# Seven block products per tile of the up projection, and the down projection as a pass of its own

## What is computed

```
u = rmsnorm(x, norm_ffn) @ ffn_w_up                  # 1024 -> 2 x 2816
u_pad = concatenate([buf0, u], axis=1)
uc = sum(u_pad[:, j:j + T] * wc[j] for j in range(3)) + ffn_conv_b
gate, up = split(uc, 2, axis=-1)
x = x + (silu(gate) * up) @ ffn_w_down               # 2816 -> 1024
x = x + sigmoid(rmsnorm(x, ple_norm) @ ple_w_gate) * (p_in @ ple_w_proj)
```

## Time and profile before

| | |
|---|---|
| median of 3 runs | 3063.3 us |
| the profiled execution | 3064.34 us |
| its span, first to last instruction | 3062.5 us |
| mean granted TensorE clock | 0.982 |
| PE / DVE / ACT / POOL busy in the span | 2942.2 / 1581.2 / 1136.7 / 141.3 us |
| matmul records | 19219 |

### The profile page before, as it was taken

How to read it: one execution, slowest core, us unless ns; L and a number is a source line. 1 busy time by engine, 2 the same in 40 slices (tenths; PEclk the granted TensorE clock), 3 DMA queues, 4 the chain that set the end, 5 groups by cost and what they waited for, 6 DMA issues and landing times. The chain is left out here.

```text
span 3062.5 us, 46703 instructions
## 1 busy us (share of the span) xinstructions
PE 2942.2 (96%) x19219; PEld 2779.4 (91%) x19219; DVE 1581.2 (52%) x2699; ACT 1136.7 (37%) x2151; POOL 141.3 (5%) x260
## 2 busy tenths in 40 slices
PE   6999989999999999999989998899999999999997
PEld 5998745999999999999989986569999999999997
DVE  5234644664544555457661446455645554455665
ACT  6233333543333223335452342344432233333353
POOL 0000300000000000000000003000000000000000
PEclk9999999999999999999999989999999999999998
DMA  3101153321111111112221022533211111111121
GB/s 131 42 28 68 73 172 118 140 74 42 44 54 42 42 55 42 56 47 83 91 72 42 17 107 84 162 103 126 74 42 42 56 42 56 42 42 46 43 98 70
DMA packets 70742, 215.40 MB, mean 70 GB/s; under 512 B 6522, under 2 KB 43386, under 8 KB 54146
## 3 DMA queue, kind: packets, MB, share of 16 engines
q1 hardware_dynamic: 70530, 212.42, 20.1%
HBM read 193.52 MB, written 18.87 MB: 69 GB/s over the span
## 5 line engine op out<-in xcount | busy, mean ns | idle before, releaser
L236 PE MATMUL psum<-h_chunk,out_weight_parts 128*128 128x352 f32 x2112 | 681.5, 323 | 0.0
L237 PE MATMUL psum<-h_chunk,out_weight_parts 128*128 128x352 f32 x2112 | 677.1, 321 | 0.0
L238 PE MATMUL psum<-h_chunk,out_weight_parts 128*128 128x352 f32 x2112 | 676.4, 320 | 0.0
L2257 DVE SCALAR_TENSOR_TENSOR conv_sum<-u_padded,vectors,conv_sum 128x1024 f32<-128x1024 f32 x176 | 226.3, 1286 | 540.5 <-ACT conv_sum L2109 537.4
L237 PEld LDWEIGHTS psum<-h_chunk,out_weight_parts 128*128 128x128 f32 x2112 | 396.8, 188 | 0.0
L236 PEld LDWEIGHTS psum<-h_chunk,out_weight_parts 128*128 128x128 f32 x2112 | 396.2, 188 | 0.0
L238 PEld LDWEIGHTS psum<-h_chunk,out_weight_parts 128*128 128x128 f32 x2112 | 395.8, 187 | 0.0
L236 PE MATMUL psum<-g_parts,out_weight_parts 128*128 128x352 f32 x960 | 309.3, 322 | 0.0
L237 PE MATMUL psum<-g_parts,out_weight_parts 128*128 128x352 f32 x960 | 309.0, 322 | 0.0
L238 PE MATMUL psum<-g_parts,out_weight_parts 128*128 128x352 f32 x960 | 308.8, 322 | 0.0
L2283 DVE TENSOR_TENSOR x<-x,psum 128x352 f32<-128x352 f32 x528 | 254.8, 519 | 94.4 <-PE psum L238 94.1
(11 more groups left out here) (360 smaller groups left out, 5420.9 us busy)
## 6 DMA issues: line engine op xcount, KB each, us to landing
out_weight_stage<-w_up_dram SPq DMA_DIRECT2D x44, 1024.0 KB, 4.7
out_weight_stage<-w_down_dram SPq DMA_DIRECT2D x22, 1024.0 KB, 4.7
mix_weight_stage<-w_in_dram SPq DMA_DIRECT2D x18, 1024.0 KB, 4.9
pages<-cache_dram SPq DMA_DIRECT2D x64, 288.0 KB, 4.3
out_weight_stage<-w_out_dram SPq DMA_DIRECT2D x16, 1024.0 KB, 6.8
out_weight_stage<-w_gate_dram SPq DMA_DIRECT2D x16, 1024.0 KB, 4.7
pages<-cache_dram SPq DMA_DIRECT2D x64, 160.0 KB, 2.6
x<-x_in_dram SPq DMA_DIRECT2D x6, 1408.0 KB, 11.2
```

The lines of the kernel that those rows point to most:

```text
L236: pe.matmul(out, lhs[0], rhs[0], start=first, stop=False)
L237: pe.matmul(out, lhs[0], rhs[1], start=False, stop=False)
L238: return pe.matmul(out, lhs[1], rhs[0], start=False, stop=last)
L2257: dve.scalar_tensor_tensor(t[:, q, 0:SEQ], row[:, tap:tap + SEQ], w, t[:, q, 0:SEQ], ALU.mult, ALU.add).then_inc(ph["conv_step"], 1)
```

## The change

**Up projection.** Tile 0 stays an ordinary product, but in 8 groups of the column slices 264, 264, 176 and 352 (`first`). For tiles 1 to 21 the product (2 x 128 rows of gate and up) x (1024 features) x (1056 tokens) is cut in two along each of the three dimensions and made from 7 block products instead of 8, a Strassen-Winograd scheme. A block product is 4 k-tiles x 3 matmuls, for each of two 264-column halves s: 24 matmuls. Four of them use sums of weight blocks (S1 to S4) and of activation blocks (T1 to T4). The T are made once per layer, in place in X, by DVE (`t_sum`), and split by ACT and DVE (`t_high`, `t_low`). The S are made per tile by POOL (`sums`), for tile 1 by DVE (`weight_sums`). Results are put together by ACT (`m1`, `corner`) and DVE (`u2`, `u3`, `c22`, `c21`, `c12`), partly by going on accumulating in the same bank. The taps are now read from u in SBUF (`taps`), u has two buffers, and the convolution of tile f - 1 runs during tile f.

**Down projection.** The gated rows go to DRAM tile by tile (`store_g`). After the last tile a separate pass goes over chunks c and output tiles t_, with all 22 k-tiles in one accumulation (`down`, 16 units of 33 matmuls per chunk, weights loaded anew for each chunk: 48 loads of 704 KB per layer). X, overwritten by the T, is stored before (`keep`) and loaded back for this pass. The order of the first four units is 0, 2, 1, 3.

**Rope scores.** All plain matmuls of a query block come first, then all rope matmuls. The slab of SBUF grows (SLAB 50304 to 54144 words), and the DMA scratch is set to 1024.

The core of the diff:

```diff
-                    w = min(512, keys - c)
-                    out = [ps[:, 2 * b + c // 512, 0:w] for b in range(2)]
+                slices = [(c, min(512, keys - c)) for c in range(0, keys, 512)]
+                for c, w in slices:
                     for b in range(2):
-                        pe.matmul(out[b], qn[:, h0 + b, queries], kn[:, h0 + b, c:c + w], start=True, stop=False)
+                        pe.matmul(ps[:, 2 * b + c // 512, 0:w], qn[:, h0 + b, queries], kn[:, h0 + b, c:c + w],
+                                  start=True, stop=False)
+                for c, w in slices:
                     for b in range(2):
-                        mm = pe.matmul(out[b], qr[part(b), h0 // 2, queries], kr[part(b), c:c + w],
-                                       start=False, stop=True)
+                        mm = pe.matmul(ps[:, 2 * b + c // 512, 0:w], qr[part(b), h0 // 2, queries],
+                                       kr[part(b), c:c + w], start=False, stop=True)
                         if c + w == keys:
                             mm.then_inc(ph["s_done"], 1)
 
...
+            def product(f, i, s, a, x, begin):
+
+                at, out = slice(s * SUB, (s + 1) * SUB), bank(i, s)
+                for k in range(KH):
+                    w = [unit(slot_of(f), a, q, k) for q in range(2)]
+                    parts = [part[:, k, at] for part in x]
+                    pe.matmul(out, w[0], parts[0], start=begin and k == 0, stop=False, skip_group_check=not begin)
+                    pe.matmul(out, w[0], parts[1], start=False, stop=False, skip_group_check=not begin)
+                    mm = pe.matmul(out, w[1], parts[0], start=False, stop=k == KH - 1, skip_group_check=not begin)
+                mm.then_inc(ph["m_done"], 1)
+
...
+            def up(f):
+                for a in product_order(f):
+                    if a == A11:
+                        pe.wait_ge(ph["w_lo_made"], 2 * f - 1)
+                    if a == S3:
+                        pe.wait_ge(ph["w_lo_made"], 2 * f)
+                        pe.wait_ge(ph["tlo_made"], 1)
+                    if a == S1:
+                        pe.wait_ge(ph["tlo_made"], 2)
+                    if a == S2:
+                        pe.wait_ge(ph["tlo_made"], 3)
+                    if a == A22:
+                        pe.wait_ge(ph["tlo_made"], 4)
+                    for s in range(2):
+                        made = 2 * (f - 1) + s + 1
+                        if a == A11:
+                            free(f, 0, s, "c11_made")
+                            product(f, 0, s, A11, block_of(0, 0), True)
+                        if a == S3:
+                            free(f, 2, s, "c21_made")
+                            product(f, 2, s, S3, t_block(T3), True)
...
+                            product(f, 1, s, S2, t_block(T2), True)
...
+                            product(f, 2, s, A22, t_block(T4), False)
+                        if a == S4:
+                            pe.wait_ge(ph["c22_made"], made)
+                            product(f, 3, s, S4, block_of(1, 1), False)
...
+            def down(d):
+                c, j = divmod(d, 2 * KX)
+                t_, half = divmod(UNIT_ORDER[j], 2)
+                if half == 0:
+                    if c:
+                        pe.wait_ge(ph["x_made"], KX * (c - 1) + t_ + 1)
+                    else:
+                        pe.wait_ge(ph[("c11_made", "u2_made", "c21_made", "c12_made")[t_ // 2]], 2 * LAST)
+                pe.wait_ge(ph["wd_lo_made"], d + 1)
+                w = wd[down_slot(d)]
+                for i in range(DK):
+                    k = half * DK + i
+                    if t_ == 0:
+                        pe.wait_ge(ph["glo_made"], groups_to(c, k))
+                    mm = product3(pe, ps[:, BANKS[t_], 0:CH], [w[:, q, i * P:(i + 1) * P] for q in range(2)],
+                                  [gd[c % 2][:, k, q, :] for q in range(2)], k == 0, k == FT - 1)
...
+            for f in range(1, FT):
+                up(f)
+            for d in range(2 * KX * NC):
+                down(d)
...
+            def sums(f):
+
+                slot, n = slot_of(f), 4 * (f - 1)
+                pool.wait_ge(ph["w_loaded"][slot], 32 * ((f - 1) // 2 + 1))
+                pool.wait_ge(ph["w_summed"], n)
+                if f >= 3:
+                    pool.wait_ge(ph["m_done"], m_before(f - 1))
+                pool.tensor_tensor(raw(slot, S1), raw(slot, S3), raw(slot, A22), ALU.add).then_inc(ph["w_summed"], 1)
+                pool.wait_ge(ph["w_summed"], n + 1)
+                pool.tensor_tensor(raw(slot, S2), raw(slot, S1), raw(slot, A11), ALU.subtract)\
+                    .then_inc(ph["w_summed"], 1)
+                pool.tensor_tensor(raw(slot, S3), raw(slot, A11), raw(slot, S3), ALU.subtract)\
+                    .then_inc(ph["w_summed"], 1)
+                pool.wait_ge(ph["w_summed"], n + 2)
+                pool.tensor_tensor(raw(slot, S4), raw(slot, A12), raw(slot, S2), ALU.subtract)\
+                    .then_inc(ph["w_summed"], 1)
 
...
+            for f in range(1, LAST):
+                store_g(f - 1)
+                if f + 2 < FT:
+                    sp.wait_ge(ph["m_done"], m_before(f) + 12)
+                    load_up(f + 2)
+            sp.wait_ge(ph["m_done"], m_before(LAST))
...
+            for c in range(NC):
+                sp.dma_start(X[:, :, chunk(c)], core.x_dram[:, :, chunk(c)]).then_inc(ph["x_back"][c], 16)
+            store_g(LAST)
...
+            t_high(T1)
+            t_high(T3)
+            first_evacuate(4)
+            first_evacuate(5)
+            t_high(T2)
+            first_evacuate(6)
+            first_evacuate(7)
+            t_high(T4)
+            act.wait_ge(ph["first_free"], FIRST_G)
+            taps(0, 1)
+            taps(0, 0)
+            for f in range(1, FT):
+                m1(f)
...
+                if f > 1:
+                    silu(f - 1)
...
+            def m1(f):
+                for s in range(2):
+                    act.wait_ge(ph["m_done"], done_after(f, A11, s))
+                    if f >= 2:
+                        act.wait_ge(ph["c12_made"], 2 * (f - 2) + s + 1)
+                    act.activation(part2[:, s], bank(0, s), ACT.Copy).then_inc(ph["m1_made"], 1)
+
...
+            def taps(f, q):
+                if f:
+                    act.wait_ge(ph["g_stored"][(f - 1) % 2], 16 * ((f - 1) // 2 + 1))
+                tile = f + q * FT
+                w2 = vec[:, ds1(tile * CONV_W + V_CW + CONV_W - 1)]
+                bias = vec[:, ds1(tile + V_CB)]
+                row = u[f % 2][:, q]
+                act.activation(t[:, q, 0:SEQ], row[:, 2:US], ACT.Identity, bias=bias, scale=w2)
+                act.activation(tokens(t[:, q, SEQ:NT]), samples(row)[:, :, CONV_W - 1:], ACT.Identity, bias=bias,
+                               scale=w2).then_inc(ph["taps_ready"], 1)
+
...
+            def t_sum(T):
+
+                n = T_ORDER.index(T)
...
+                dve.wait_ge(ph["nlo_made"], 16)
+                for j in range(0, KH, 2):
...
+                    if n:
+                        dve.wait_ge(ph["t_summed"], 2 * (n - 1) + j // 2 + 1)
+                    dve.tensor_tensor(rows((kh, out)), rows(left), rows(right), ALU.subtract)\
+                       .then_inc(ph["t_summed"], 1)
+
+            def t_low(T):
+                later = {T1: 3, T3: 2, T2: 4, T4: 4}
+                dve.wait_ge(ph["thi_made"], T_ORDER.index(T) + 1)
+                dve.wait_ge(ph["t_summed"], 2 * later[T])
+                dve.tensor_tensor(t_rows(tl, T), t_rows(X, T), th[:, T].bitcast(F32), ALU.subtract)\
+                   .then_inc(ph["tlo_made"], 1)
+
...
+            def u2(f, s):
+                dve.wait_ge(ph["m1_made"], 2 * (f - 1) + s + 1)
+                dve.wait_ge(ph["m_done"], done_after(f, S2, s))
+                dve.tensor_tensor(part2[:, s], part2[:, s], bank(1, s), ALU.add).then_inc(ph["u2_made"], 1)
+
+            def u3(f, s):
+                dve.wait_ge(ph["m_done"], done_after(f, S3, s))
+                dve.wait_ge(ph["u2_made"], 2 * (f - 1) + s + 1)
+                if f >= 2:
+                    dve.wait_ge(ph["c22_made"], 2 * (f - 1))
+                dve.tensor_tensor(part3[:, s], part2[:, s], bank(2, s), ALU.add).then_inc(ph["u3_made"], 1)
+
...
+            sums_low(1)
+            t_low(T3)
+            t_sum(T2)
+            t_low(T1)
+            t_sum(T4)
+            t_low(T2)
+            t_low(T4)
+            u2(1, 0)
+            u2(1, 1)
+            u3(1, 0)
+            u3(1, 1)
+            c22(1, 0)
+            c22(1, 1)
+            blocks_low(2)
+            dve.wait_ge(ph["zeroed"], 4)
...
+            for f in range(2, FT):
+                if f == 2:
+                    gated(0)
+                conv(f - 1, 1, 0)
+                conv(f - 1, 1, 1)
+                u2(f, 0)
+                conv(f - 1, 0, 0)
+                u2(f, 1)
+                conv(f - 1, 0, 1)
```

(3 more changed lines are left out.)

774 lines of the change are left out of this document (506 added, 268 removed).

## The result

The changed kernel takes 3032.2 us (median of 4, 3028.8 to 3036.4) against 3063.1: ratio 0.9899, 95% interval [0.9882, 0.9916]. It is faster, by 31 us where 67 were forecast, and 6 us outside the range. A second set of runs gave 0.9882 [0.9867, 0.9897].

The account below looks back on a forecast made before the run. PE's matmul time was taken to bound the network. Per layer: -49.0 products, +15.1 entry, +1.5 turn, -0.3 boundary; twice that, less 1.5 for rope, is -66.9 from 3064.3: 2997.4 profiled, 2996 median, range 2966 to 3026 us.

Parts of the forecast that it names:

- The price of a 264-column matmul: Feed-forward network on PE: 0.1224 us per matmul, from a line through 256 and 352 columns.
- the gain of the steady tiles: Up projection: a tile falls from 22.92 to 20.56 us, so 21 tiles give -49.6 us per layer.
- rival (c): Up projection: 264-column matmuls hardly cheaper than 352-column ones, as weight loads set the pace; 3095 us, chance 0.03.
- rival (b): Every up-projection tile: DVE late at u3, so A22 waits; 2.7 us in each of 42 tiles, 3109 us, chance 0.06.
- the wait of A12: Tile 1: A12 waits 6.2 us for m1, which stands on ACT behind the last t_high and taps(0).
- S1's: Tile 1: block product S1 waits 4.1 us for the low part of T1, with POOL's sums in between.
- tile 2, which its margin just takes: Entry: DVE runs some 3 us behind its timetable in tile 2, absorbed by its margin; no added time.
- 0 beyond that: Down pass: no loss beyond the turn's 1.5 us, since weights and rows need 190 GB/s; other end +3.
- the turn that was forecast at 1.5: Turn to the down pass: the third unit waits for down_low(2) on DVE, +1.5 us per layer.
- rival (d): Down pass or turn starved by reloaded weights: a third of a us in each of 96 units, 3028 us, chance 0.08.
- Tile 0's slice of 176 columns: Tile 0 on PE: 0.0855 us per 176-column matmul, within a tile of 23.5 us, +0.6.
- The rope order: Attention scores: two switches fewer in 16 blocks, worth 0 to 6.4 us; -1.5 us taken.

Follow-up runs that it names:

- Conv_early: Changed kernel with tile 0's convolution moved ahead of u2 in tile 1 on DVE and its SiLU product into tile 1: 3005.9 us, 0.9810 of the kernel before.
- gate_late: Changed kernel with tile 0's convolution moved ahead of u2 in tile 1, its SiLU product left at the head of tile 2: 3011.6 us, one run.
- g_first: Changed kernel with the third chunk's first two g loads issued ahead of two down units instead of behind them: 3016.4 us, 0.9840 of the kernel before.
- sums_inside: Changed kernel with the last norm sums inside tile 0's second group and the transposes inside its third: 3031.9 us, 0.9890 of the kernel before.
- five_edits: Changed kernel with earlier m1, later POOL sums, tile 0's convolution and product in tile 1, norm sums inside a group, late X read: 3001.9 us.

## Why the prediction was right and wrong

**Right.** The sign. The price of a 264-column matmul: 0.1224 forecast, and 19 tiles of 168 at 20.473 us each make 0.1219, so the gain of the steady tiles is there, and rival (c) is out. No wait inside a steady tile, though POOL's sums and the convolution do hold each other up: rival (b) is out. In tile 1, the wait of A12 (6.5 for 6.2, for `m1`) and that of A22 (1.0 for 0.9) came as named. S1's came at 1.6 instead of 4.1 and S3's hardly at all, because tile 0 had already taken up 4.5 us more than its sum: tile 0 and tile 1 together are 61.4 us where 60.1 were forecast, and that they come out so near is two misses that cancel.

**Wrong: "tile 2, which its margin just takes".** This is the step that failed, 10.4 us a layer, some 23 for both with the second layer's 33.0. I carried a lateness of 3 us forward as a number and did not write out tile 2. In the trace the first u2 is 9.8 us behind the timetable (17.1 for 7.3), so A12 waits 3.0 and A22 5.5, and half clock adds 1.5. The convolution of tile 0 stands last in DVE's order, and `taps(f)` carry a wait for the store of g that the prediction never mentions, although the change adds it. Conv_early shows that the whole 10.4 go when this chain starts earlier, and gate_late that 2.7 of them come back with a late product alone; how the other 7.8 divide between DVE's work and its standing still, no run separates.

**Wrong: the down pass's "0 beyond that".** I compared rates (190 GB/s asked, 381 seen), and g_first, which moves the same bytes, shows that the rate did not cause the long wait. What was not written out is the order of SP, and behind it of ACT and DVE, at the turn of a chunk. The 9.5 of the first layer are 6.3 of waits, of which g_first removes the 4.3 and of which 1.2 are the turn that was forecast at 1.5, some 3 of half clock after it (what is left of 263.2 after the waits and 1584 steps of 0.1603, as in g_first), and 1.7 by that step instead of 0.1592, less the 1.5 that were forecast. The result lands near rival (d)'s 3028, but not by its mechanism of weights that come too slowly.

**Mis-sized.** Tile 0's slice of 176 columns (0.0855 by a line through 256 and 352 columns, 0.111 measured: 1.2 us). The norm's wait (1.4) and its clock (1.6) were left out; sums_inside shows that tile 1 would have eaten them. The rope order: -1.5 taken, -6.4 measured with an interval of -3.7 to -9.2. The prediction had a bound of 6.4 and stayed near the other end, on a guess about the next softmax step that no row supported. This miss made the total look better by some 5 us.

**The range.** Its top end stood 15 us a layer above the forecast. Tile 2 and the down pass, some 10 us each in both layers, exceed that. A new order across five queues deserved more than one entry in the sum for "everything else".

## What to carry to other kernels

Where a change introduces a steady loop, its steady state is the easy part: write out the first two rounds and every turn of a chunk, queue by queue, until the lateness is gone. For each new wait, ask when the thing waited for can start, not only how long it takes. Then look up the time of the longest wait before designing a test for it; the test of a wait at the wrong place cost a run and taught only that.

## What the runs showed of the hardware

- The step of a matmul does not fall in a line with its columns: 0.160 us at 352, 0.122 at 264, 0.119 at 256, 0.111 at 176. From 352 to 264 a column is worth 0.43 ns, from 256 to 176 only 0.10. No width between 176 and 256 was measured. The 176 are one stretch of 48 matmuls at a granted clock of 1.00; in conv_early they take the same 5.2 us from first to last.
- The same wait of 1.41 us in tile 0 was followed by steps of 0.22 us in the changed kernel (its window 646 to 651 had a granted clock of 0.66) and by none in conv_early (1.00, 24 steps in 2.99 us), though no edit of conv_early stands ahead of it. So a gap of this size costs clock in some executions and not in others: tile 0 is 28.9 or 27.4 us.
- POOL and DVE also held each other up where DVE ran two-input operations with a column scalar (five_edits, 686 to 690): beside POOL's sums a convolution of 1024 elements took 2.37 us instead of 1.28 and one of 32 elements 1.24 instead of 0.25.
